# Scores of two soft heads issued together, one on each half of the partitions, at every second step

## The reference, cut to what matters

```
scores = jnp.einsum('bnqhd,bnkhd->bhnqk', qc, kband) * (1.0 / math.sqrt(d))
scores = scores + bias[None, :, None, :, :]
p = jax.nn.softmax(scores, axis=-1)
o = jnp.einsum('bhnqk,bnkhd->bnqhd', p, vband)
...
s = jnp.einsum('bqhcd,bkhcd->bhcqk', qi, k).astype(f32)
p = jax.nn.softmax(s, axis=-1)
```

## Time and profile before

| what | value |
|---|---|
| median of three runs | 2541.82 us (2538.09 to 2541.99) |
| profiled execution, span | 2537.0 us |
| TensorE matmul busy | 2482.8 us, 98% |
| TensorE weight loads busy | 2093.9 us, 83% |
| VectorE busy | 1716.6 us, 68% |
| ScalarE busy | 1439.1 us, 57% |
| HBM | 218 GB/s over the span |

### The profile page before, as it was taken

The page is one execution under the profiler, slowest core; times in us unless marked ns, Lnnn a source line. Parts: engine busy times, 40 slices in busy tenths (PEclk is TensorE's granted clock), DMA queues, the critical chain, the costliest instruction groups (busy, mean ns, idle before and its releaser), DMA issues. The chain is left out here.

```text
span 2537.0 us, 33705 instructions
## 1 busy us (share of the span) xinstructions
PE 2482.8 (98%) x13444; PEld 2093.9 (83%) x13444; DVE 1716.6 (68%) x1892; ACT 1439.1 (57%) x1603; POOL 80.1 (3%) x94
## 2 busy tenths in 40 slices
PE   8999999899999999999999999999999999999998
PEld 6889978787888888888777789878888788887887
DVE  5565465788898898888975754566556665557554
ACT  5344353588888888888855444454444544445442
POOL 0000010000000000000000200000000000002000
PEclk9999999999999999999999999999999999999999
DMA  8155551599999999999955165542555255552552
GB/s 304 66 197 202 183 187 69 206 352 348 344 338 343 334 346 348 325 349 343 347 189 187 69 221 185 172 169 100 204 187 181 71 197 183 183 174 83 191 183 100
DMA packets 241907, 555.49 MB, mean 219 GB/s; under 512 B 10760, under 2 KB 36768, under 8 KB 241440
## 3 DMA queue, kind: packets, MB, share of 16 engines
q1 hardware_dynamic: 241696, 552.40, 62.5%
HBM read 551.29 MB, written 1.07 MB: 218 GB/s over the span
## 5 line engine op out<-in xcount | busy, mean ns | idle before, releaser
L1822 DVE TENSOR_TENSOR wlo<-raw,whi 128x2048 fp32r<-128x2048 f32 x488 | 1119.0, 2301 | 476.5 <-ACT whi L1452 475.3
L1452 ACT ACTIVATE whi<-raw 128x2048 fp32r<-128x2048 f32 x488 | 935.4, 1923 | 579.5 <-issue 155.5
L931 PE MATMUL bank<-xt_hi,whi 128*128 128x256 f32 x1056 | 299.1, 283 | 0.0
L931 PE MATMUL bank<-xt_hi,wlo 128*128 128x256 f32 x1056 | 298.9, 283 | 0.0
L931 PE MATMUL bank<-xt_lo,whi 128*128 128x256 f32 x1056 | 298.9, 283 | 0.0
L777 PE MATMUL bank<-whi,xt_hi 128*128 128x512 f32 (+1 forms) x528 | 204.4, 387 | 6.2 <-DVE wlo L1828 3.0
L931 PEld LDWEIGHTS bank<-xt_lo,whi 128*128 128x128 f32 x1056 | 202.6, 192 | 1.3
L931 PEld LDWEIGHTS bank<-xt_hi,whi 128*128 128x128 f32 x1056 | 202.6, 192 | 1.3
L931 PEld LDWEIGHTS bank<-xt_hi,wlo 128*128 128x128 f32 x1056 | 202.6, 192 | 0.0
L777 PE MATMUL bank<-wlo,xt_hi 128*128 128x512 f32 (+1 forms) x528 | 198.2, 375 | 0.0
L777 PE MATMUL bank<-whi,xt_lo 128*128 128x512 f32 (+1 forms) x528 | 198.2, 375 | 0.0
(11 more groups left out here) (304 smaller groups left out, 4098.3 us busy)
## 6 DMA issues: line engine op xcount, KB each, us to landing
raw<-in_moe_wg SPq DMA_DIRECT2D x88, 1024.0 KB, 5.9
raw<-in_moe_wu SPq DMA_DIRECT2D x88, 1024.0 KB, 5.7
raw<-in_moe_wd SPq DMA_DIRECT2D x88, 1024.0 KB, 5.5
raw<-in_mlp_w_up SPq DMA_DIRECT2D x64, 1024.0 KB, 5.4
raw<-in_mlp_w_down SPq DMA_DIRECT2D x64, 1024.0 KB, 4.8
raw<-in_diff_w_in SPq DMA_DIRECT2D x24, 1024.0 KB, 5.3
raw<-in_w_in SPq DMA_DIRECT2D x19, 1024.0 KB, 8.3
raw<-in_moba_w_in SPq DMA_DIRECT2D x12, 1024.0 KB, 5.1
```

Of the source, the lines that this page charges most:

```text
L931: mm = pe.matmul(bank[b + f // 2][:, f % 2 * S:(f % 2 + 1) * S], w[:, k, f * P:(f + 1) * P], a[:, kx, :], start=(kx == 0 and i == 0 and f ...
L1452: act.activation(whi[u % NH][:, :], raw[u % NR][:, :], ACT.Copy).then_inc(hi_ready[u % NR], 2)
L1822: dve.tensor_tensor(wlo[u % NR][:, :], raw[u % NR][:, :], whi[u % NH][:, :].bitcast(F32), ALU.subtract).then_inc(lo_ready[u % NR], 2)
```

## The change

The scores of heads i-1 and i are issued at odd steps only, by a new function `pair_scores`: the 128-column matmul of the even head, that of the odd head, then the 256-column matmuls of both, and in hybrid layers the four bias matmuls behind them. One `start=True` opens each bank, so the second matmul of a bank now has `start=False`. Before the pair TensorE waits until VectorE has read both earlier heads (`z_read` g instead of g-1). VectorE reduces both heads at the odd step and then writes `nmx`: in one instruction for the two heads, in layer 4 in two. ScalarE's program, the projection parts and the turns are as they were.

```diff
-                    j = i - 1
-                    if 0 <= j < n:
-                        g = HEAD0[l] + NSTICK[kind] + j
-                        pe.wait_ge(qk_ready, g // 2 + 1)
-                        if g >= 2:
-                            pe.wait_ge(z_read, g - 1)
...
-                        mm.then_inc(scored, 1)
+                    if i % 2 == 1 and i < n:
+                        pair_scores(l, i - 1)
...
+            def pair_scores(l, j):
+
+                kind = KIND[l]
+                g = HEAD0[l] + NSTICK[kind] + j
+                pe.wait_ge(qk_ready, g // 2 + 1)
+                if g >= 2:
+                    pe.wait_ge(z_read, g)
+                heads = [(bank[h], head_qk(l, NSTICK[kind] + j + h)) for h in range(2)]
+                for b, q in heads:
+                    pe.matmul(b[:, 0:P], q[:, 0:P], q[:, 2 * P:3 * P], start=True, stop=False, skip_group_check=True)
+                for b, q in heads:
+                    mm = pe.matmul(b[:, P:3 * P], q[:, P:2 * P], q[:, 2 * P:4 * P], start=False, stop=kind != HYB,
+                                   skip_group_check=True)
+                    if kind != HYB:
+                        mm.then_inc(scored, 1)
+                if kind == HYB:
+                    pe.wait_ge(got["toep"], 16 * (l + 1))
+                    for h, (b, _) in enumerate(heads):
+                        pe.matmul(b[:, 0:P], flip8, toep[:, j + h, P:2 * P], start=False, stop=False,
+                                  skip_group_check=True)
+                        pe.matmul(b[:, P:3 * P], flip8, toep[:, j + h, :], start=False, stop=True,
+                                  skip_group_check=True).then_inc(scored, 1)
...
-                        dve.wait_ge(z_read, g + 1)
...
+                    if i % 2 == 1 and i < n:
+                        for j in (i - 1, i):
+                            g, s = HEAD0[l] + NSTICK[kind] + j, SOFT0[l] + j
+                            dve.wait_ge(scored, g + 1)
...
+                        else:
+                            dve.tensor_scalar(nmx[:, :, i - 1:i + 1], mx[:, :, i - 1:i + 1], -1.0, None,
+                                              ALU.mult).then_inc(nmx_ready, 2)
```

More of the change, by code:

```diff
@@ L2136, in soft_heads @@
                         finish_group(l, 5, False)
[L2137 to L2146, removed]
+                    if i % 2 == 1 and i < n:
+                        for j in (i - 1, i):
+                            g, s = HEAD0[l] + NSTICK[kind] + j, SOFT0[l] + j
+                            dve.wait_ge(scored, g + 1)
+                            if s >= 4:
+                                dve.wait_ge(pt_done, s - 3)
+                            for t, c in enumerate((slice(0, P), slice(P, 3 * P))):
+                                ins = dve.tensor_tensor_reduce(z[:, s % 4, c], bank[g % 2][:, c], mask[:, c], SCALE,
+                                                               -3e38, ALU.add, ALU.max, mx[:, t, j:j + 1])
+                            ins.then_inc(z_read, 1)
                         dve.wait_ge(z_read, g + 1)
                         if kind == SWA:
-                            dve.tensor_scalar(nmx[:, :, j], mx[:, :, j], sinks[:, j:j + 1], -1.0, ALU.max,
-                                              ALU.mult).then_inc(nmx_ready, 1)
-                        else:
-                            dve.tensor_scalar(nmx[:, :, j], mx[:, :, j], -1.0, None, ALU.mult).then_inc(nmx_ready, 1)
+                            for j in (i - 1, i):
+                                dve.tensor_scalar(nmx[:, :, j], mx[:, :, j], sinks[:, j:j + 1], -1.0, ALU.max,
+                                                  ALU.mult).then_inc(nmx_ready, 1)
+                        else:
+                            dve.tensor_scalar(nmx[:, :, i - 1:i + 1], mx[:, :, i - 1:i + 1], -1.0, None,
+                                              ALU.mult).then_inc(nmx_ready, 2)
                     if i < late_parts(l):
```

## The result

The changed kernel takes 2527.11 us, the median of four runs (2523.16 to 2529.56), against 2540.32 (2538.09 to 2541.99) for the kernel before beside it: a ratio of 0.9946 [0.9935, 0.9958]. It is faster, by 13.2 us. The forecast was 2511 us with a range from 2502 to 2524, so the direction was right and the time was outside the range. The profiled execution has a span of 2527.8 us (2529.56 in all), 9.2 less than the profiled one of before.

The account below looks back on a forecast made before the run. TensorE, busy 98% of the span, was taken as the bound, VectorE in the tails of layers 2 and 5. Savings of 13.0 + 6.8 + 5.0 + 5.8 = 30.6 us off 2541.8 gave 2511 us, range 2502 to 2524.

Parts of the forecast that it names:

- the end of a stage: Layers 3 and 4: last head scored one step sooner, its exponential wait of 0.66 mostly goes; 1.0 us more each.
- The pair: Scores of two heads on opposite array halves take 0.86 us, 0.97 with entry, against 1.92: 0.95 saved per pair.
- Strict order: Rival: within a pair matmuls start only in program order, 1.07 us instead of 0.86; 2517 us in all, chance 0.12.
- taking turns: Rival: the two halves do not run at once, a pair takes 1.6 to 1.8 us; about 2535 us, chance 0.06.
- Covered pairs: 14 pairs in projection steps of layers 2 to 5, each saving 0.95: 13.3 us (3.8 per layer, 1.9 in layer 4).
- Hybrid layers: Two hybrid layers: first two pairs save 1.75 each, the last costs 0.35, longer waits 0.2; 2.9 us per layer, 5.8 together.
- Tail of layers 2 and 5: VectorE bounds; L845 can start when split L1846 ends, no longer waiting for the last head: 2.7 us per layer.
- Tail of layers 3 and 4: After waits for VectorE's copy a pair saves 0.5 (layer 3) or 0.35 us (layer 4): 2.0 and 2.1, plus 1.0 each.
- the tails give nothing: Rival: latency through VectorE eats every tail pair, leaving 13.3 and 3.5 us saved; 2525 us, chance 0.1.

Follow-up runs that it names:

- the second set: The changed kernel run again without any edit, for the spread: 2524.15 us, 0.9934 of the kernel before.
- the fill: The changed kernel plus matmuls nobody reads, issued where TensorE waits in layer 3 (steps 8, 12) and layer 4 (step 8): 2520.93 us, 0.9922 of the kernel before.
- the head-by-head pair: The changed kernel, but TensorE issues all of one head's matmuls in a pair and then the other's, instead of alternating: 2523.93 us, 0.9936 of the kernel before.
- tails alone: The changed order only in tail steps, single heads as before in steps with a projection part: 2542.37 us, 1.0007 of the kernel before.
- covered alone: The changed order only in steps with a projection part, single heads as before in the tails: 2521.76 us, 0.9921 of the kernel before.

## Why the prediction was wrong

Two steps failed. The first is the list of what VectorE does in a tail between a pair's scores and the copy of p: it left out the half units of `lo`, and TensorE waits 2.36, 1.68 and 1.37 us where 0.4 to 0.6 was charged. The second is the end of a stage: the forecast had the last head's exponential off the path (1.0 us in each of layers 3 and 4, most of the 2.7 in layers 2 and 5), and TensorE still waits for it. On top of both came a granted clock that the sum took as full.

The stages again, with what the runs have for each term (us saved; "full clock" is the stage in an execution without falls in it: layers 0 and 1 from the second set, layer 4 from the fill with its five unread matmuls, layer 3 from the head-by-head pair):

| stage | forecast | full clock | profile after |
|---|---|---|---|
| layers 0 and 1, each | 2.9 | 3.6 | 2.1, 1.9 |
| layers 2 and 5, each | 6.5 | 5.2 | 5.2 |
| layer 3 | 6.8 | 2.4 | -1.3 |
| layer 4 | 5.0 | 2.2 | 1.1 |
| sum | 30.6 | 22.2 | 14.2 |

- **The pair: right.** 0.86, and 0.86 in the other order too. Strict order and taking turns are both refuted. In a tail the pair takes less off TensorE, though: with tails alone its busy time falls from 52.24 to 49.26 in layer 3 (four pairs) and from 41.38 to 36.61 in layer 4 (six), 0.75 to 0.8 a pair where 0.95 was counted. Why is open.
- **Covered pairs: right in layer 2, half in layer 4.** 4.3 in layer 2 (covered alone) where 3.8 was counted. In layer 4 0.9 for 1.9, with the wait of 0.93 behind a half unit of `lo` shown above. It looks like the failed step once more, but no run moved this half unit, so it is not shown.
- **Hybrid layers: right, low.** The pair and its four bias matmuls take 2.27 us (416.49 to 418.76) where 2.34 was counted (2.45 less the entry), and the stage gains 3.6 instead of 2.9. The time from the last scores to L845 was to stay 8.6; in the second set, at full clock, it is 7.9 (414.70 to 422.58), which is the difference.

```profile
416.49 0.49 PE L1366 MATMUL bank<-qk 64*128 64x128 f32 x4
...
417.35 0.49 PE L1375 MATMUL bank<-toep,cst 128*128 128x128 f32 x2
...
418.76 0.49 PE L1342 MATMUL bank<-cst,z 128*128 128x128 f32 x3
```

- **Tail of layers 2 and 5: mis-sized.** Forecast 2.7, measured 0.9. VectorE was counted well: the split that was to let L845 start ends at about 1410.3 after a stage start at 1359.57, 50.7 into the stage, where the count had 50.1 to 50.8 (1414.8 to 1415.5, less 1360.90 and the 3.8 of the covered pairs). What failed is the sentence "the last head ... is no longer what L845 waits for":

```profile
1407.67 1.06 ACT L1480 ACTIVATE xt_hi<-bank 128x512 fp32r<-128x512 f32 x2
...
1408.62 0.40 ACT L1581 ACTIVATE z<-z,nmx 128x128 f32<-128x128 f32 x1
...
1409.03 1.28 DVE L1854 TENSOR_TENSOR xt_lo<-bank,xt_hi 128x512 fp32r<-128x512 f32 x2
...
1409.65 0.55 PE L1342 MATMUL bank<-cst,z 128*128 128x128 f32 x3 [0.90 <-ACT z L1583]
...
1411.47 0.71 PE L845 MATMUL bank<-whi,xt_hi 128*128 128x512 f32 x2
```

TensorE still waits 0.90 for the last head's exponential (1.05 before), and L845 stands behind that head's turn and products. The split is ready 1.2 us before L845. The exponential itself (L1581, L1583) stands in ScalarE's queue behind the split `xt_hi`. I had looked only at VectorE's chain, and the end was ScalarE's. This is read from the profile; no run changes it.
- **Tail of layers 3 and 4: the failed step.** I charged the waits at 0.4 to 0.6 for the pair's own latency. With the half units out of the way that is about right: 0.57, 0.16 and 0.59 are left in layer 3 (half units later), and 0.27 at layer 4's regular steps, though 0.69 and 0.71 at two others. But the list of what VectorE does between scores and copy left out the half units of `lo`, though they were in the description of the step. Two in layer 3 and one in layer 4 now stand ahead of two reductions and the copy: waits of 2.36 and 1.68, and in layer 4 this one, ahead of a regular one:

```profile
1977.58 0.43 PE L1389 MATMUL bank<-h_qkv,pt 128*128 128x64 f32 x2 [1.37 <-DVE pt L2171]
...
1986.43 0.44 PE L1389 MATMUL bank<-h_qkv,pt 128*128 128x64 f32 x2 [0.27 <-DVE pt L2171]
```

  With the half units moved behind the copy and nothing else changed, layer 3 goes to 47.35: 5.6 saved of the 6.8. What is still missing fits the end of the stage: the wait of 0.66 for the last exponential, of which the forecast said that it mostly goes, is 0.66 again (1712.20 in that profile). In layer 4 39.91 is 2.5 of the 5.0. TensorE's busy time there falls by 6.3 where eight pairs of 0.95 are 7.6, and its idle time rises from 1.02 to 4.85: 4.0 of it are eight waits for the copy, the longest the 0.91 behind the covered pair, and 0.85 is the last exponential's (0.81 before).
- **The granted clock: a term that was not in the sum.** The forecast took the full clock of the page before for granted. Between the full-clock sum (22.2) and the gain in span of the two profiles (9.2) lie 13 us: 8.0 inside the stages, by the table, and 5 outside them, where the profile has the falls at 368, 460 and 2000 us. But that sets a profile with many falls against one with none but the end, and the median of the kernel before, from which the forecast started, has its usual falls in it already. The mean clock of every execution is on record, so the clock's part can be estimated: call span times (1 - mean clock) the clock time lost. Among executions of one kernel, one that lost 1 us more took 0.6 us longer (0.5 to 0.7; a fit over 105 executions of twelve kernels). With this price the changed kernel would be 20.7 us faster than before (19.1 to 22.5) if both had a mean clock of 0.999, close to the sum of the stages, and its lower clock takes back 5 us of that (2.5 to 7.3). The fit does not say what made the clock fall. Shown by an experiment is the part in layers 3 and 4: 3.2 us in the median and the spread of 9.8.

So of the 30.6 forecast some 8 to 10 us were never there (the failed and mis-sized terms), about 5 went to the clock, and 15 to 16 is what eight executions show against 39 of before; the four of the first set happened to be slower, with 13.2. The range's upper end held the case "the tails give nothing" (2525), which is close to what came, but for other reasons, and I had given it 0.1: VectorE's 94% in the earlier trace rows spoke for it in layer 2, and it was layer 3, which I named as the evidence against it, that lost most.

What stays open is when the clock falls. In the kernel with covered pairs alone, layer 3 spends 23.9 us at the lower level behind this stretch, in which TensorE was busier than in the stretches shown above:

```profile
1695.70:1699.10 3.40, 2.51 (x17) 1.74 (x17) 2.45 (x13) 2.28 (x9) 0.00 (x0) 1.00 0.03 7
1699.10:1723.00 23.90, 23.90 (x95) 19.63 (x96) 10.98 (x41) 8.05 (x26) 0.00 (x0) 0.50 0.00 0
```

The other three runs of that kernel are 7.7 to 9.1 us faster than the profiled one, so it is not a fixed property of the schedule. And the head-by-head pair had 5.30 us of idle in the same stage and no fall. In the one profile of it, filling the idle time left no fall in layers 3 and 4; which idle time brings one, and why not every time, these runs do not say.

## What to carry to other kernels

When an engine's work is gathered from every step into every second one, go through every *other* instruction in its queue and ask whether it now stands in front of the doubled piece; here a piece that was free between two single ones cost its full length, and the wait of its own producer too, and in layer 3 moving it one step brought more (3.2 us at full clock) than the change itself (2.4). A matmul saved on TensorE in a stretch bound by latency turns into idle time, and idle time can cost a second time through the clock: price a tail once with full clock and once with a fall behind each of its longer waits. Ask for the end of a stage on every engine's chain, not only on the one that looked busiest before.

## What the hardware showed unexpectedly

- Two heads of four matmuls each on opposite halves of the rows take 0.86 us in whichever order they are issued, against 0.85 for one head: a full factor of two even when the second head stands entirely behind the first.
- Adding 19 unread matmuls to idle stretches made the kernel about 3 us faster in the median (the intervals overlap), and the spread of four runs was 2.2 us instead of 9.8.
- Falls of the granted clock to 1.2 GHz in the middle of a stage lasted 3.4 and 6.8 us, once 17.1 and once 23.9, with TensorE busy nearly throughout (16.5 us of the 17.1, all of the 23.9), and some of them came in one execution and not in the next of the same kernel.
